# Three-block transformer in one Trainium2 kernel: the second half of the compressed keys and values computed inside the attention's first steps

## The chip, the cores and the metric

The kernel runs on one core of a Trainium2 chip. The metric is the device time of one execution in microseconds. The kernel before was timed three times: 2164.24, 2169.11 and 2172.72 us, median 2169.11 us. TensorE (PE) multiplies, VectorE (DVE) and ScalarE (ACT) work element by element, GpSimd (POOL) and SyncE (SP) mostly issue transfers here. Each engine runs its own program in order, and the programs meet at semaphores.

## The reference, cut to what matters

The input is 512 tokens of 1024 features. Three blocks follow one another: a mixed recurrent and linear-attention block, a retention block, and a block with native sparse attention (NSA); each ends with a feed-forward layer. Everything is float32. The change is in the shared keys and values of the third block and in the start of its attention:

```
kv = rms_norm_2(h, kv_norm) @ kv_w
k_c, v_c, k_s, v_s, k_w, v_w = [t.reshape(B, S, G, d) for t in jnp.split(kv, 6, axis=-1)]

def compress(t, pe, w1, w2):              # t: 512 tokens, 4 groups, 64 features
    blocks = t[:, blk_idx] + pe[:, None, :]           # 31 overlapping windows of 32 tokens, step 16
    blocks = blocks.transpose(0, 1, 3, 2, 4).reshape(B, n_cmp, G, CMP_LEN * d)
    return jax.nn.silu(blocks @ w1) @ w2              # 2048 -> 256 -> 64

kc = compress(k_c, cmp_pe_k, cmp_w1_k, cmp_w2_k)
vc = compress(v_c, cmp_pe_v, cmp_w1_v, cmp_w2_v)
```

The attention then has three branches per head: over the 31 compressed keys (kc, vc), over selected blocks, and over a window; each is a masked softmax with a relative bias, and sigmoid gates weigh their sum. With 512 tokens the selected blocks and the window cover all keys before the query, so both are dense causal attentions. Heads: 16 in 4 groups of 64 features.

## The kernel before, in words

Features lie on partitions, so activations are tiles of 128 features by 512 tokens. Every matrix product is made in three passes of float32r: each operand is split into a high part and a low rest (AH and AL of the input, WH and WL of the weights), and a "part" is the three matmuls AH·WH, AL·WH and AH·WL of one 128x128 weight block (L413 for feature tiles, L462 for token tiles). A tile has 8 parts, 24 matmuls.

Weights come in units of 512 KB. SP loads a unit into RAW (three slots), ACT copies it to WH (L883), DVE subtracts and writes WL (L1319). `ahead(u)` makes these copies up to unit u; `before(name, m)` is `ahead` of that tile's unit plus LOOK = 2. ACT may write WH of unit v only when PE has finished unit v-3.

The plan gives each tile one of PSUM banks 0 to 3 in turn. Its order here is: `kv_t` 0 to 7 (features of k_c, v_c, and of k_s and k_w), `kv_v` (tokens: v_s and v_w; four banks at once), `nsa_t` 8 (gates), `nsa_t` 0 to 7 (queries, two heads to a tile; 1 to 7 in bank 7). A tile enters its bank only when the former tenant was read out (L394).

- The evacuation of `kv_t` 0 to 3 (L1376) writes CK. `kv_t` 4 to 7 go to T[n % 4], ACT and DVE spread each over KHH and KLL (L1205 to L1206, L1799 to L1800).
- DVE sets KCH, KCL and VC to zero ahead of CK (L1782 and L1783).
- `windows(i)` (L1803) builds X2, the blocks of half i: eight copies of 64x496 (L1812) and then one addition of the position embedding to all of X2 (L1816). Half 0 is made between `kv_tile(5)` and `kv_tile(6)` in DVE's program, half 1 after `kv_v`. 
- `hidden(i)` (L734) is blocks @ w1: 32 float32 matmuls of 124 columns, each of which leaves two records. `hidden_act(i)` (L1227) is the SiLU on ACT, `compressed(i)` (L749, L751) the product with w2. Half 0 stands between `kv_v` and `nsa_t` 8, half 1 between `nsa_t` 8 and `nsa_t` 0. POOL loads the second w1 into the same W1 when hidden(0) is done (L379).
- DVE copies the compressed values into VC (L1839).

The attention is a loop of steps written out by hand, the same step number s on PE, ACT and DVE (L845, L1252, L1952). Step s is one head, one block of 128 queries (order 0, 3, 1, 2) and one branch: steps 0 to 3 have 128 keys, 4 to 7 512, 8 to 11 256, 12 to 15 384. In step s PE transposes the weights of step s-9 (`turn`, L821, banks 2, 3 and 6 in rotation), computes the scores of s (L806 and L807, banks 0 and 1 in rotation), and every fourth step from 14 on the values (L839). DVE adds the bias and takes the maximum (L1927) into the ring SS, ACT takes the exponential (L1267), DVE weighs (L1950) the step s-6, ACT copies turned weights (L1259). The compressed branch has its own small scores (L791 and L792, 16 pairs), first in step 2. Parts of the next query tile are spread over steps: parts 4 to 7 of `nsa_t` 1 in steps 0 to 3, `nsa_t` 2 in steps 6 to 13. `query(n)` on DVE (L1845, L1852) and `query_high(n)` on ACT (L1203) turn a query tile into QHL: n = 1 stands in step 4, n = 2 in step 15. Ahead of the loop DVE also makes the gates (L1857, L1860) and a memset of CS8 (L1863).

Of the kernel before, what the change touches and what calls it, by code (L numbers as in the profile page):

```python
# [14 lines left out]
S = 512  # L15
# [7 lines left out]
LOOK = 2  # L23
# [6 lines left out]
    ("gla_norm", 1), ("pe_k", 16), ("pe_v", 16),  # L30
# [46 lines left out]
def plan():  # L77
    p = Plan()
    for m in OPEN_IN + (11, 8, 9, 2, 3):
        p.tile("w_in_t", m)  # L80
    p.tokens("w_in_v", 0)
    for m in (12, 13, 14, 15, 4, 5, 6, 7):
        p.tile("w_in_t", m)
    for m in range(8):
        p.tile("w_out", m)

    def ffn(n):
        for m in range(44):
            p.tile(f"ffn{n}_in", m)
        for m in range(8):  # L90
            p.tile(f"ffn{n}_out", m)

    ffn(1)
    for h in range(4):
        for m in range(4):
            p.tile("ret_t", 8 * h + m)
        p.tokens("ret_v", h)
        for j in range(4):
            p.bank["scores", h, j] = p.turn()
        for m in range(4, 8):  # L100
            p.tile("ret_t", 8 * h + m)
    for m in range(8):
        p.tile("ret_out", m)
    ffn(2)
    for m in range(8):
        p.tile("kv_t", m)
    p.tokens("kv_v", 0)
    for m in (8, 0):
        p.tile("nsa_t", m)
    for m in range(1, 8):  # L110
        p.tile("nsa_t", m, bank=7)
    for m in range(8):
# [33 lines left out]
def build(nc, D, out):  # L146
    p = plan()
    n_units = len(p.units)
    with ExitStack() as ctx:
# [24 lines left out]
        sb("origin", [128, 96])  # L174
# [41 lines left out]
        with ExitStack() as ar:  # L216
            TT = [sb(f"TT{i}", [128, 4, S], stack=ar) for i in range(2)]
            KHH = sb("KHH", [128, 8, S], F32R, ar)
            KLL = sb("KLL", [128, 8, S], F32R, ar)
            VS = sb("VS", [128, 4, 512], stack=ar)  # L220
            GT = sb("GT", [128, 4, 48], stack=ar)
            KCH = sb("KCH", [128, 4, 32], F32R, ar)
            KCL = sb("KCL", [128, 4, 32], F32R, ar)
            VC = sb("VC", [128, 4, 4, 64], stack=ar)
            with ExitStack() as ac:
                CK = sb("CK", [128, 4, S], stack=ac)
                X2 = sb("X2", [128, 16, 124], stack=ac)
                W1 = sb("W1", [128, 16, 256], stack=ac)
                HC = sb("HC", [128, 2, 124], stack=ac)
                W2 = sb("W2", [128, 2, 2, 128], stack=ac)  # L230
            QHL = [sb(f"QHL{i}", [128, 4, S], F32R, ar) for i in range(2)]
            SS = [sb(f"SS{i}", [128, S], stack=ar) for i in range(8)] + SQ
            PT = [sb(f"PT{i}", [128, S], stack=ar) for i in range(5)] + [ACC]
            NM = sb("NM", [128, 8], stack=ar)
            SM = sb("SM", [128, 4, 4], stack=ar)
            CF = sb("CF", [128, 4, 4], stack=ar)
            CM = sb("CM", [128, 3, 8], stack=ar)
# [73 lines left out]
        def query_after(s):  # L311

            return {4: 1, 15: 2}.get(s, s // PAIR + 1 if 2 * PAIR <= s <= 6 * PAIR and s % PAIR == 0 else None)

        def queries_before(s):

            return {4: 2}.get(s, s // PAIR + 2 if PAIR <= s < 6 * PAIR and s % PAIR == 0 else None)

        def queries_in(s):

            if s < 4:
                return 1, s + 4
# [28 lines left out]
        def pool_program(e):  # L351
# [36 lines left out]
        def tensor_program(e):  # L388
# [338 lines left out]
            def hidden(i):  # L727
                for ht in range(2):
                    enter(4 + ht, ("hidden", i, ht))
                    if ht == 0:  # L730
                        e.wait_ge(s_w1, 16 * (i + 1))
                        e.wait_ge(*kv_v.at(("x2", i)))
                    for lp in range(16):
                        t = e.matmul(BANK[4 + ht][:, 0:124], W1[:, lp, ht * 128:ht * 128 + 128], X2[:, lp, :],  # L734
                                     start=lp == 0, stop=lp == 15)
                    t.then_inc(matmul.did(("hidden", i, ht)))

            def compressed(i):
                b = 6 + i
# [26 lines left out]
            for kk in range(4):  # L766
                part("nsa_t", 1, kk, A)
# [77 lines left out]
            for s in range(LAST):  # L845
                if TURN <= s < N + TURN:
                    turn(s - TURN)
                if s < N:
                    scores(s)
                for f in range(8):  # L850
                    if s == small_at(f):
                        small_scores(f)
                    if s == small_at(f) + 7:
                        small_turn(f)
                if s >= VALUES and (s - VALUES) % 4 == 0:
                    values((s - VALUES) // 4)
                if queries_in(s):
                    part("nsa_t", *queries_in(s), A)
# [12 lines left out]
        def scalar_program(e):  # L871
# [360 lines left out]
            e.wait_ge(*set_v.at("kc"))  # L1232
# [5 lines left out]
            hidden_act(1)  # L1238

            def query_high(n):  # L1240
                g = n // 2
                e.wait_ge(*free_v.at(("nsa_t", n)))
                if g > 1:
                    e.wait_ge(*matmul.at(("att", GROUP * (g - 1) - 1)))
# [4 lines left out]
            e.wait_ge(*matmul.at(("cmp", 1)))  # L1249
            query_high(0)  # L1250
            before("nsa_t", 1)
            for s in range(LAST + 3):  # L1252
# [8 lines left out]
                if s < N:  # L1261
# [47 lines left out]
        def vector_program(e):  # L1309
# [471 lines left out]
            for k in (KCH, KCL):  # L1781
                e.memset(k[:, :, :].bitcast(F32), 0.0).then_inc(set_v.did("kc"))  # L1782
            e.memset(VC[:, :, :, :], 0.0).then_inc(set_v.did("vc"))  # L1783

# [18 lines left out]
            def windows(i):  # L1803

                for g in range(4):
                    e.wait_ge(*free_v.at(("kv_t", 2 * i + g // 2)))
                    for par in range(2):
                        src = CK[64 * (g % 2):64 * (g % 2) + 64, 2 * i + g // 2, :]
                        win = bass.AP(src.tensor, src.offset + par, [src.ap[0], [2, 16], [16, 31]])
                        if i == 1 and g == 0 and par == 0:  # L1810
                            e.wait_ge(*matmul.at(("hidden", 0, 1)))
                        e.tensor_copy(X2[64 * par:64 * par + 64, :, 31 * g:31 * g + 31], win).then_inc(  # L1812
                            kv_v.did(("pairs", i)))
                pe = V("pe_k" if i == 0 else "pe_v", 0, 16).rearrange("p (l o) -> p l o", o=1)
                e.wait_ge(*kv_v.at(("pairs", i)))
                e.tensor_tensor(X2[:, :, :], X2[:, :, :], pe.broadcast_to([128, 16, 124]), ALU.add).then_inc(  # L1816
                    kv_v.did(("x2", i)))

            for n in range(6):
                kv_tile(n)  # L1820
            windows(0)
            kv_tile(6)
            kv_tile(7)
            before_tokens("kv_v", 0)
            for f in range(8):
                low("q", f, "mix_pre1")
            windows(1)
# [8 lines left out]
            e.wait_ge(*matmul.at(("cmp", 1)))  # L1836
            e.wait_ge(*set_v.at("vc"))
            for i in range(4):
                e.tensor_copy(VC[32 * i:32 * i + 31, i, :, :],  # L1839
                              BANK[7][0:31, 0:256].rearrange("p (g d) -> p g d", g=4)).then_inc(free_v.did(("cmp", 1)))  # L1840

            def query(n):
# [13 lines left out]
            e.wait_ge(*matmul.at("gates"))  # L1856
            e.tensor_copy(GT[:, :, :], BANK[6][:, 0:192].rearrange("p (a b) -> p a b", a=4)).then_inc(  # L1857
                free_v.did("gates"))
            e.wait_ge(*free_v.at("gates"))
            e.reciprocal(GT[:, :, :], GT[:, :, :]).then_inc(set_v.did("gates"))  # L1860
            before("nsa_t", 1)
            e.wait_ge(*kv_v.at(("k", 3)))
            e.memset(CS8, NEG).then_inc(set_v.did("small"))  # L1863
# [15 lines left out]
            def small_scores(f):  # L1879
# [4 lines left out]
                e.wait_ge(*set_v.at("small"))  # L1884
# [176 lines left out]
def laid_out(inp):  # L2061
# [13 lines left out]
        "pe_k": a["cmp_pe_k_2"].reshape(16, 128).T, "pe_v": a["cmp_pe_v_2"].reshape(16, 128).T,  # L2075
    }
# [56 lines left out]
```

## Time and profile before

| what | value |
|---|---|
| median of three runs | 2169.11 us (2164.24 to 2172.72) |
| profiled execution | 2173.35 us, its span 2171.5 us |
| PE busy | 2088.9 us (96%) |
| DVE busy | 1033.1 us (48%) |
| ACT busy | 820.2 us (38%) |
| POOL busy | 12.7 us (1%) |
| mean granted TensorE clock | 0.978 |
| chain that ended last | PE 88%, DVE 6%, ACT 4%, issue 1% |

The span is the time from the first to the last instruction; the execution takes 1.85 us more than that. Times in the rows are microseconds from the span's start. `[1.74 <-DVE CK L1376]` behind a row says that the engine stood idle for 1.74 us before it, and that a write of CK by DVE at line 1376 released it. Ends of matmuls are modelled: a matmul of 512 columns is shown as 0.39 us, while the next starts 0.227 us after it. The granted clock has two levels, 1.00 (2.4 GHz) and 0.50 (1.2 GHz).

### The profile page before, as it was taken

Reading aid. Unit: us, or ns where it says so; the run is one execution under the profiler, and the core shown is the slowest. Engines: PE = TensorE matmul, PEld = TensorE weight load, DVE = VectorE, ACT = ScalarE, POOL = GpSimd, SP = SyncE. Lnnn points to the kernel's source line nnn. Section 1 sums busy time; section 2 is a strip of 40 time slices with the busy share of each in tenths; the row PEclk is TensorE's granted clock in tenths of the full one; section 3 lists DMA queues with packets and bytes.
Section 4 is the critical chain, followed back from the end, with each engine's and each line's share of the span. In section 5 each row is a group of like instructions: output and inputs, shape, how many; then the busy total and the mean of one; then the engine's idle time right before and its main releaser. Section 6 shows DMA issues by size and latency. Waiting matters only on the chain.

```text
span 2171.5 us, 25460 instructions
## 1 busy us (share of the span) xinstructions
PE 2088.9 (96%) x10172; PEld 1711.2 (79%) x10172; DVE 1033.1 (48%) x1705; ACT 820.2 (38%) x1290; POOL 12.7 (1%) x24
## 2 busy tenths in 40 slices
PE   7799999999999999999999999999899999999997
PEld 6578788888887787788788888777788778888886
DVE  4645444443344353342644442275677635444323
ACT  4563333333323233233433322234577634333221
POOL 0000000000000000000000000000000000000000
PEclk9999999999999999999999999999899999999998
DMA  4212233333331221223232333433111022332331
GB/s 134 68 59 78 85 100 97 97 92 100 100 104 45 92 97 54 87 88 97 68 97 97 97 92 97 131 102 107 40 40 40 3 86 78 97 97 97 90 97 66
DMA packets 51812, 184.38 MB, mean 85 GB/s; under 512 B 5818, under 2 KB 6090, under 8 KB 51440
## 3 DMA queue, kind: packets, MB, share of 16 engines
q1 hardware_dynamic: 49248, 171.99, 25.4%
q0 software_dynamic: 2160, 10.63, 1.5%
q8 instruction: 81, 1.33, 0.2%
q14 instruction: 35, 0.29, 0.0%
q10 hardware_dynamic: 288, 0.15, 0.0%
HBM read 180.61 MB, written 2.14 MB: 84 GB/s over the span
## 4 chain that ended last, share of the span: by engine, by line
PE 88%; DVE 6%; ACT 4%; issue 1%; DMA 0%; SPq 0%; DVEq 0%; ACTq 0%
PE bank L413 71%; PE bank L462 6%; PE bank L839 2%; PE bank L700 1%; DVE WL L1319 1%; PE bank L821 1%; PE bank L806 1%; PE bank L690 1%; PE bank L807 1%; PE bank L513 1%; ACT WH L883 1%; PE bank L479 1%; PE bank L596 0%; DVE MF L1650 0%; DMA RAW<-in_w_in_t 0%
## 5 line engine op out<-in xcount | busy, mean ns | idle before, releaser
L1319 DVE TENSOR_TENSOR WL<-RAW,WH 128x1024 fp32r<-128x1024 f32 (+1 forms) x326 | 391.5, 1205 | 579.8 <-ACT WH L883 579.0
L413 PE MATMUL bank<-AH,WH 128*128 128x512 f32 x1584 | 628.4, 400 | 25.7 <-ACT AH L893 15.5
L413 PE MATMUL bank<-AL,WH 128*128 128x512 f32 x1584 | 622.5, 396 | 3.5 <-DVE AL L1337 3.5
L413 PE MATMUL bank<-AH,WL 128*128 128x512 f32 x1584 | 618.9, 394 | 1.9 <-DVE WL L1319 1.9
L883 ACT ACTIVATE WH<-RAW 128x1024 fp32r<-128x1024 f32 (+1 forms) x326 | 338.1, 1041 | 583.6 <-PE bank L413 503.7
L413 PEld LDWEIGHTS bank<-AH,WH 128*128 128x128 f32 x1584 | 302.2, 191 | 94.1 <-issue 20.4
L413 PEld LDWEIGHTS bank<-AL,WH 128*128 128x128 f32 x1584 | 301.8, 191 | 69.6 <-DVE AL L1337 9.6
L413 PEld LDWEIGHTS bank<-AH,WL 128*128 128x128 f32 x1584 | 302.3, 191 | 66.7 <-DVE WL L1319 2.8
L413 PE MATMUL bank<-HH,WL 128*128 128x512 f32 x528 | 205.4, 389 | 0.0
L413 PE MATMUL bank<-HH,WH 128*128 128x512 f32 x528 | 205.4, 389 | 0.0
L413 PE MATMUL bank<-HLO,WH 128*128 128x512 f32 x528 | 205.4, 389 | 0.0
L1376 DVE TENSOR_TENSOR T<-bank,RS 128x512 f32<-128x512 f32 x156 | 106.6, 686 | 162.0 <-PE bank L413 162.0
L413 PEld LDWEIGHTS bank<-HH,WH 128*128 128x128 f32 x528 | 99.1, 188 | 20.7
L413 PEld LDWEIGHTS bank<-HH,WL 128*128 128x128 f32 x528 | 99.1, 188 | 20.6
L413 PEld LDWEIGHTS bank<-HLO,WH 128*128 128x128 f32 x528 | 99.1, 188 | 20.5
L1096 ACT ACTIVATE T<-T 128x512 f32<-128x512 f32 x66 | 41.7, 632 | 127.2 <-DVE T L1376 127.2
L1101 ACT ACTIVATE HH<-T 128x512 fp32r<-128x512 f32 x66 | 41.7, 632 | 125.8 <-DVE T L1622 125.8
L462 PE MATMUL bank<-WH,AH 128*128 128x512 f32 x192 | 76.2, 397 | 6.6 <-DVE XP L1376 4.4
L462 PE MATMUL bank<-WL,AH 128*128 128x512 f32 x192 | 75.8, 395 | 1.6 <-DVE WL L1319 1.6
L462 PE MATMUL bank<-WH,AL 128*128 128x512 f32 x192 | 75.7, 394 | 0.0
L1267 ACT ACTIVATE SS<-SS,NM 128x128 f32<-128x128 f32 (+3 forms) x104 | 58.1, 559 | 28.9 <-DVE NM L1927 28.4
L1624 DVE TENSOR_TENSOR HLO<-T,HH 128x512 fp32r<-128x512 f32 x66 | 45.7, 693 | 46.1 <-ACT HH L1101 46.1
(300 smaller groups left out, 2249.1 us busy)
## 6 DMA issues: line engine op xcount, KB each, us to landing
RAW<-in_ffn_in SPq DMA_DIRECT2D x132, 512.0 KB, 3.5
RAW<-in_ffn_out SPq DMA_DIRECT2D x48, 512.0 KB, 3.5
RAW<-in_ret_t SPq DMA_DIRECT2D x32, 512.0 KB, 3.6
RAW<-in_ffn_out SPq DMA_DIRECT2D x24, 384.0 KB, 3.1
RAW<-in_w_in_t SPq DMA_DIRECT2D x17, 512.0 KB, 3.6
RAW<-in_ret_v SPq DMA_DIRECT2D x16, 512.0 KB, 3.6
RAW<-in_ret_out SPq DMA_DIRECT2D x16, 512.0 KB, 3.6
RAW<-in_nsa_t SPq DMA_DIRECT2D x9, 512.0 KB, 3.5
```

The costliest lines, as they stand in the source:

```text
L413: t = e.matmul(BANK[b][:, :], wt[:, sl], xx[:, slot(kk) if name == "nsa_out" else kk, :], start=kk == 0 and n == 0, stop=kk == kt - 1 and ...
L462: t = e.matmul(BANK[b][:, :], xx[:, kk, tt * 128:(tt + 1) * 128], wt[:, sl], start=kk == 0 and n == 0, stop=kk == 7 and n == 2)
L479: t = e.matmul(BANK[4][:, 4 * tt + q:4 * tt + q + 1], SQ[1][:, ROWS[tt]], ones[:, :], start=True, stop=True)
L513: t = e.matmul(BANK[5][:, ROWS[tt]], src[:, at + tt:at + tt + 1].broadcast_to([128, 128]), ident[:, :], start=True, stop=True)
L839: e.matmul(out[hh], VS[:, j, c:c + 64], PT[(4 * u + 2 * br + hh) % NPT][:, ROWS[j]], start=br == 0 and j == 0, stop=False)
L883: e.activation(WH[v % W_SLOTS][:, 0:n], RAW[v % RAW_SLOTS][:, 0:n], ACT.Copy).then_inc(w_high.did(v))
L1096: e.activation(a[:, :], a[:, :], ACT.Silu).then_inc(gate_a.did((n, j)))
L1101: e.activation(HH[n][:, j, :], T[2 * (j % 2)][:, :], ACT.Copy).then_inc(hid_a.did((n, j)))
L1267: e.activation(scores, scores, ACT.Exp, bias=NM[:, s % 8:s % 8 + 1], scale=-1.0, accum_out=SM[:, u % 4, 2 * hh + br:2 * hh + br + 1]).then ...
L1319: e.tensor_tensor(WL[w][:, 0:n], RAW[r][:, 0:n], WH[w][:, 0:n], ALU.subtract).then_inc(w_low.did(v))
L1376: e.tensor_tensor(dst, BANK[p.bank[name, m]][:, :], RS[:, :], ALU.mult).then_inc(free_v.did((name, m)))
L1624: e.tensor_tensor(HLO[n][:, j, :], a[:, :], HH[n][:, j, :], ALU.subtract).then_inc(hid_v.did((n, j)))
```

## The change

1. `kv_t` 4 and 5 go to banks 6 and 7. So the turn of banks 0 to 3 moves by two for everything behind them: `kv_t` 6 and 7 get banks 1 and 2, `kv_v` 3, 0, 1, 2, `nsa_t` 8 and 0 banks 3 and 0, `nsa_out` and the last feed-forward layer are moved by two as well.
2. The zeroes of KCH, KCL, VC and the memset of CS8 go from DVE to POOL.
3. The blocks of half 0 are built after `kv_tile(7)`, one group at a time between the weight units of `kv_v`. Copy and addition become one instruction: eight additions of 64x496 per half. For it the vector table has two more entries of 16 columns, the embeddings with their halves swapped.
4. hidden(1) is issued in steps 0 to 5 of the attention, six matmuls in each (two in step 5); compressed(1) in step 9, into bank 5; ACT's hidden_act(1) in step 7; DVE's copies to VC in step 11. compressed(0) stays where it was. 
5. `nsa_t` 1 is computed whole ahead of the loop. `query(1)` moves from step 4 to 3, `query(2)` from 15 to 14; `before("nsa_t", 1)` to step 1, `before("nsa_t", 2)` from step 4 to 7. The gates are made in step 2 on DVE.
6. HC and W2 no longer share room with the later buffers; the ring SS has 9 buffers, not 10.

```
-            p.tile("kv_t", m)
+            p.tile("kv_t", m, bank={4: 6, 5: 7}.get(m))
...
-                HC = sb("HC", [128, 2, 124], stack=ac)
-                W2 = sb("W2", [128, 2, 2, 128], stack=ac)
...
-            SS = [sb(f"SS{i}", [128, S], stack=ar) for i in range(8)] + SQ
+            SS = [sb(f"SS{i}", [128, S], stack=ar) for i in range(6, 9)]
+            SS = [sb(f"SS{i}", [128, S], stack=ar) for i in range(4)] + SQ + SS
+            HC = sb("HC", [128, 2, 124], stack=ar)
+            W2 = sb("W2", [128, 2, 2, 128], stack=ar)
...
         def query_after(s):
...
-            return {4: 1, 15: 2}.get(s, s // PAIR + 1 if 2 * PAIR <= s <= 6 * PAIR and s % PAIR == 0 else None)
+            return {3: 1, 14: 2}.get(s, s // PAIR + 1 if 2 * PAIR <= s <= 6 * PAIR and s % PAIR == 0 else None)
...
         def queries_before(s):
...
-            return {4: 2}.get(s, s // PAIR + 2 if PAIR <= s < 6 * PAIR and s % PAIR == 0 else None)
+            return {1: 1, 7: 2}.get(s, s // PAIR + 2 if PAIR <= s < 6 * PAIR and s % PAIR == 0 else None)
...
         def queries_in(s):
...
-            if s < 4:
-                return 1, s + 4
...
             e.dma_start(W2[:, :, :, :], D["cmp_w2"]).then_inc(s_w2, 16)
+            for k in (KCH, KCL):
+                e.memset(k[:, :, :].bitcast(F32), 0.0).then_inc(zeroed.did("kc"))
+            e.memset(VC[:, :, :, :], 0.0).then_inc(zeroed.did("vc"))
...
+            e.wait_ge(*kv_v.at(("k", 3)))
+            e.memset(CS8, NEG).then_inc(zeroed.did("small"))
             e.wait_ge(*matmul.at(("hidden", 0, 1)))
...
-            hidden(0)
+            for ht in range(2):
+                hidden(0, ht, range(16))
             compressed(0)
-            q_split = split_of("q")
-            tile("nsa_t", 8, A, q_split)
-            hidden(1)
-            compressed(1)
+            tile("nsa_t", 8, A, split_of("q"))
             tile("nsa_t", 0, A)
...
-            for kk in range(4):
-                part("nsa_t", 1, kk, A)
+            tile("nsa_t", 1, A)
...
+                if s < 6:      
+                    for lp in range(6 * s, min(6 * s + 6, 32)):
+                        hidden(1, lp // 16, (lp % 16,))
+                if s == 9:
+                    compressed(1)
...
-            hidden_act(1)
...
                 e.wait_ge(*free_v.at(("nsa_t", n)))
+                if n == 0:
+                    e.wait_ge(*kv_v.at(("x2", 1)))
...
+                if s == 7:
+                    hidden_act(1)
...
-                        e.tensor_copy(X2[64 * par:64 * par + 64, :, 31 * g:31 * g + 31], win).then_inc(
-                            kv_v.did(("pairs", i)))
-                e.tensor_tensor(X2[:, :, :], X2[:, :, :], pe.broadcast_to([128, 16, 124]), ALU.add).then_inc(
-                    kv_v.did(("x2", i)))
+                        e.tensor_tensor(X2[64 * par:64 * par + 64, :, 31 * g:31 * g + 31], win,
+                                        pe.rearrange("p (l o) -> p l o", o=1).broadcast_to([64, 16, 31]),
+                                        ALU.add).then_inc(kv_v.did(("x2", i)))
-            for n in range(6):
+            for n in range(8):
                 kv_tile(n)
-            windows(0)
-            kv_tile(6)
-            kv_tile(7)
-            before_tokens("kv_v", 0)
+            for g in range(4):
+                ahead(p.first["kv_v", 0] + g + LOOK)
+                windows(0, (g,))
...
+                if s == 2:
+                    gates()
+                if s == 11:
+                    compressed_values()
```

## Rows read from the trace of the kernel before

**Rows 1.** The page, part 4: the chain that ended last, by engine.
```profile
PE 88%; DVE 6%; ACT 4%; issue 1%; DMA 0%; SPq 0%; DVEq 0%; ACTq 0%
```

**Rows 2.** Timeline of PE, kv_t and kv_v: start, length, instruction, count [idle before <-releaser].
```profile
1440.26 1.98 PE L413 MATMUL bank<-AH,WL 128*128 128x512 f32 x8
1443.98 0.50 PE L413 MATMUL bank<-AH,WH 128*128 128x512 f32 x1 [1.74 <-DVE CK L1376]
...
1468.12 0.50 PE L462 MATMUL bank<-WL,AH 128*128 128x512 f32 x1 [1.63 <-DVE WL L1319]
...
1474.30 0.50 PE L462 MATMUL bank<-WH,AH 128*128 128x512 f32 x1 [2.23 <-DVE T L1376]
```

**Rows 3.** Timeline of DVE in the same stretch.
```profile
1442.47 0.91 DVE L1783 MEMSET VC<- 128x1024 f32 x1 [0.16 <-issue]
...
1459.56 5.12 DVE L1812 COPY X<-CK 64x496 f32<-64x496 f32 x8
1464.71 2.23 DVE L1816 TENSOR_TENSOR X<-X,vec 128x1984 f32<-128x1984 f32 x1
...
1473.56 0.68 DVE L1376 TENSOR_TENSOR T<-bank,RS 128x512 f32<-128x512 f32 x1
```

**Rows 4.** Timeline of PE from hidden(0) to step 11.
```profile
1492.12 7.30 PE L734 MATMUL bank<-X,W 128*128 128x124 f32 x64
...
1507.58 7.38 PE L734 MATMUL bank<-X,W 128*128 128x124 f32 x64 [0.20 <-issue]
1515.42 1.05 PE L751 MATMUL bank<-W,HC 128*31 128x64 f32 x16 [0.46 <-ACT HC L1227]
...
1525.32 0.22 PE L806 MATMUL bank<-KHH,QHL 128*128 128x128 f32 x1
...
1528.24 0.33 PE L806 MATMUL bank<-KHH,QHL 128*128 128x128 f32 x1 [0.94 <-DVE NM L1927]
...
1530.27 0.48 PE L413 MATMUL bank<-AH,WH 128*128 128x512 f32 x1
...
1539.18 0.79 PE L806 MATMUL bank<-KHH,QHL 128*128 128x512 f32 x1 [3.22 <-DVE NM L1927]
...
1548.20 0.27 PE L821 MATMUL bank<-ident,SS 128*128 128x128 f32 x1
```

**Rows 5.** Timeline of DVE, VC to step 5.
```profile
1516.51 1.75 DVE L1839 COPY VC<-bank 31x256 f32<-31x256 f32 x4 [7.72 <-PE bank L751]
...
1525.33 1.35 DVE L1860 RECIPROCAL GT<-GT 128x192 f32<-128x192 f32 x1
...
1534.08 0.69 DVE L1845 SCALAR_TENSOR_TENSOR T<-bank,RS 128x512 f32<-128x512 f32 x1
1535.56 1.41 DVE L1852 TENSOR_TENSOR QHL<-T,QHL 64x512 fp32r<-64x512 f32 x2 [0.80 <-ACT QHL L1203]
1537.30 1.23 DVE L1319 TENSOR_TENSOR WL<-RAW,WH 128x1024 fp32r<-128x1024 f32 x1 [0.33 <-ACT WH L883]
```

**Rows 6.** Timeline of ACT: table load, SiLU, weight copy, exponential.
```profile
1509.48 1.28 ACT L1227 ACT_TABLE_LOAD   x1
1511.43 0.27 ACT L1227 ACTIVATE HC<-bank 128x124 f32<-128x124 f32 x1 [0.67 <-PE bank L734]
...
1536.21 1.06 ACT L883 ACTIVATE WH<-RAW 128x1024 fp32r<-128x1024 f32 x1
...
1539.88 0.71 ACT L1267 ACTIVATE SS<-SS,NM 128x512 f32<-128x512 f32 x1
```

**Rows 7.** Stretches: us, busy PE, PEld, DVE, ACT, POOL (count), granted clock, DMA share, GB/s.
```profile
1534.00:1540.00 6.00, 2.78 (x8) 1.85 (x8) 4.81 (x12) 4.16 (x9) 0.00 (x0) 0.78 0.09 10
1540.00:1550.00 10.00, 10.00 (x50) 8.54 (x50) 6.75 (x30) 5.18 (x17) 0.00 (x0) 0.74 0.13 48
...
1600.00:1620.00 20.00, 19.39 (x167) 15.94 (x161) 16.13 (x55) 15.78 (x44) 0.00 (x0) 1.00 0.09 27
```

**Rows 8.** Timeline of POOL, the memset at the start.
```profile
0.74 0.95 POOL L352 MEMSET bd<- 128x1024 f32 x1 [0.29 <-POOLq L2125]
```

More of the change, by code:

```diff
@@ L29 @@
     ("conv_w", 16), ("conv_b", 4), ("lru_ba", 4), ("lru_bi", 4), ("lru_lambda", 4), ("b_alpha", 2),
-    ("gla_norm", 1), ("pe_k", 16), ("pe_v", 16),
+    ("gla_norm", 1), ("pe_k", 16), ("pe_v", 16), ("pe_k_swapped", 16), ("pe_v_swapped", 16),
 ]
@@ L173, in build @@
         sums = sb("sums", [128, 4])
-        sb("origin", [128, 96])
+        sb("origin", [128, 64])
         BANK = [ctx.enter_context(nc.psum_tensor(f"bank{i}", [128, 512], F32)) for i in range(8)]
@@ L725, in tensor_program, with hidden @@
             tokens("kv_v", 0, A)
[L727 to L736, printed above, removed]
+            def hidden(i, ht, lps):
+                b = 4 + ht
+                for lp in lps:
+                    if lp == 0:
+                        enter(b, ("hidden", i, ht))
+                        if ht == 0:
+                            e.wait_ge(s_w1, 16 * (i + 1))
+                            e.wait_ge(*kv_v.at(("x2", i)))
+                    t = e.matmul(BANK[b][:, 0:124], W1[:, lp, ht * 128:ht * 128 + 128], X2[:, lp, :], start=lp == 0,
+                                 stop=lp == 15)
+                    if lp == 15:
+                        t.then_inc(matmul.did(("hidden", i, ht)))
             def compressed(i):
-                b = 6 + i
+                b = 6 - i
                 enter(b, ("cmp", i))
@@ L1231, in scalar_program @@
             e.wait_ge(*matmul.at(("cmp", 0)))
-            e.wait_ge(*set_v.at("kc"))
+            e.wait_ge(*zeroed.at("kc"))
             e.activation(KCH[:, :, 0:31], BANK[6][:, 0:128].rearrange("p (g n) -> p g n", g=4)[:, :, 0:31],
@@ L1248, in scalar_program @@
             before("nsa_t", 0)
-            e.wait_ge(*matmul.at(("cmp", 1)))
             query_high(0)
-            before("nsa_t", 1)
             for s in range(LAST + 3):
@@ L1778, in vector_program @@
             fourth("kv_t", 3, "kv", False)
-            for k in (KCH, KCL):
-                e.memset(k[:, :, :].bitcast(F32), 0.0).then_inc(set_v.did("kc"))
-            e.memset(VC[:, :, :, :], 0.0).then_inc(set_v.did("vc"))
             def kv_tile(n):
@@ L1801, in kv_tile, with windows @@
                         kv_v.did(("k", k)))
-            def windows(i):
-                for g in range(4):
+            def windows(i, gs):
+                for g in gs:
                     e.wait_ge(*free_v.at(("kv_t", 2 * i + g // 2)))
+                    own = slice(64 * (g % 2), 64 * (g % 2) + 64)
                     for par in range(2):
-                        src = CK[64 * (g % 2):64 * (g % 2) + 64, 2 * i + g // 2, :]
+                        src = CK[own, 2 * i + g // 2, :]
                         win = bass.AP(src.tensor, src.offset + par, [src.ap[0], [2, 16], [16, 31]])
+                        pe = V(("pe_k", "pe_v")[i] + ("" if g % 2 == par else "_swapped"), 0, 16)[own]
                         if i == 1 and g == 0 and par == 0:
                             e.wait_ge(*matmul.at(("hidden", 0, 1)))
-                        e.tensor_copy(X2[64 * par:64 * par + 64, :, 31 * g:31 * g + 31], win).then_inc(
-                            kv_v.did(("pairs", i)))
-                pe = V("pe_k" if i == 0 else "pe_v", 0, 16).rearrange("p (l o) -> p l o", o=1)
-                e.wait_ge(*kv_v.at(("pairs", i)))
-                e.tensor_tensor(X2[:, :, :], X2[:, :, :], pe.broadcast_to([128, 16, 124]), ALU.add).then_inc(
-                    kv_v.did(("x2", i)))
-            for n in range(6):
+                        e.tensor_tensor(X2[64 * par:64 * par + 64, :, 31 * g:31 * g + 31], win,
+                                        pe.rearrange("p (l o) -> p l o", o=1).broadcast_to([64, 16, 31]),
+                                        ALU.add).then_inc(kv_v.did(("x2", i)))
+            for n in range(8):
                 kv_tile(n)
-            windows(0)
-            kv_tile(6)
-            kv_tile(7)
-            before_tokens("kv_v", 0)
+            for g in range(4):
+                ahead(p.first["kv_v", 0] + g + LOOK)
+                windows(0, (g,))
             for f in range(8):
                 low("q", f, "mix_pre1")
-            windows(1)
+            windows(1, range(4))
             e.wait_ge(*kv_a.at("kc"))
@@ L1835, in vector_program, with compressed_values @@
                 free_v.did(("nsa_t", 8)))
[L1836 to L1840, printed above, removed]
+            def compressed_values():
+                e.wait_ge(*matmul.at(("cmp", 1)))
+                e.wait_ge(*zeroed.at("vc"))
+                for i in range(4):
+                    e.tensor_copy(VC[32 * i:32 * i + 31, i, :, :],
+                                  BANK[5][0:31, 0:256].rearrange("p (g d) -> p g d", g=4)).then_inc(free_v.did(("cmp", 1)))
             def query(n):
@@ L1855, in vector_program, with gates @@
             query(0)
[L1856 to L1863, printed above, removed]
+            def gates():
+                e.wait_ge(*matmul.at("gates"))
+                e.tensor_copy(GT[:, :, :], BANK[6][:, 0:192].rearrange("p (a b) -> p a b", a=4)).then_inc(
+                    free_v.did("gates"))
+                e.wait_ge(*free_v.at("gates"))
+                e.reciprocal(GT[:, :, :], GT[:, :, :]).then_inc(set_v.did("gates"))
             def by_head(t):
@@ L1883, in small_scores @@
                 e.wait_ge(*matmul.at(("small", f)))
-                e.wait_ge(*set_v.at("small"))
+                e.wait_ge(*zeroed.at("small"))
                 if f > 0:
@@ L2075, in laid_out @@
         "pe_k": a["cmp_pe_k_2"].reshape(16, 128).T, "pe_v": a["cmp_pe_v_2"].reshape(16, 128).T,
+        "pe_k_swapped": a["cmp_pe_k_2"].reshape(16, 2, 64)[:, ::-1].reshape(16, 128).T,
+        "pe_v_swapped": a["cmp_pe_v_2"].reshape(16, 2, 64)[:, ::-1].reshape(16, 128).T,
     }
```

## The prediction

> **What bounds the kernel now.** Read the chain of the page first: PE holds 88% of what ended last, DVE 6% [rows 1]. Shortening DVE or ACT work is worth only what it takes from PE's waits, so the next view is PE's timeline around the edits, with the idle time in brackets. Between the last matmul of `kv_t` 3 and hidden(0) PE waits three times: 1.74 us for the evacuation of bank 1 (CK), 1.63 us for WL, 2.23 us for the evacuation of `kv_t` 7's bank [rows 2]. In the attention's first steps it waits 0.94 and 3.22 us for DVE's maximum [rows 4]. The stretches then show what a timeline hides: from 1534 to 1540 PE is busy 2.78 of 6 us, and its granted clock is 0.78 there and 0.74 in the next 10 us, against 1.00 in the running attention [rows 7]. Everything behind step 11 I expect to shift as a block.
>
> **kv_t and kv_v (edits 1 to 3).** PE issues 96 matmuls of `kv_t` 4 to 7 and 96 of `kv_v` between 1442.24 (1440.26 + 1.98) and 1492.12: 49.9 us [rows 2, 4]. The last 78 of them run without a wait from 1474.30 to 1492.12, 17.82 us, with 0.11 us for the restart: 0.227 us each [rows 2, 4]. 192 x 0.227 = 43.6 us. So 6.3 us can go. Does it?
> - `kv_t` 4 enters bank 6, which no one has read from lately, and its weight rests are written ahead: no wait, so DVE's memsets (0.91 us for VC, two more of some 0.17) and the CK evacuations no longer stand in the way [rows 3]. On POOL the same size took 0.95 us [rows 8]; there it runs behind the load of w1, while PE is at the sums after the feed-forward, some 35 us ahead of the first use. The bounds are 0 and, if POOL disturbed DVE for all three, 1.3 us; I take 0.
> - The windows no longer precede the weight rest of `kv_v` 0: DVE goes from `kv_tile(5)` straight to it and writes it near 1459, PE needs it at 1442.1 + 96 x 0.227 = 1463.9. Before, 5.12 + 2.23 us stood ahead of it [rows 3].
> - `kv_v`'s first two bank groups use banks 3 and 0, long read out; the third and fourth use those of `kv_t` 6 and 7 and begin 2.7 and 4.1 us after 1463.9, and DVE reads `kv_t` 7 out by about 1465.5. No wait.
> - What is late next: X2. One addition of 64x496 I take at 0.67 us, just under the 0.68 us of 512 columns [rows 3]; no row shows it with this stepped source and broadcast vector; the ends are 0.64 (5.12 / 8, the copy of that shape) and 1.31 (copy and addition one behind the other). ACT can write the weight unit of `nsa_t` 0 only when PE has done the third unit of `kv_v`, 1463.9 + 16.3 = 1480.2; 1.06 us for it, 1.23 for DVE's rest [rows 5, 6], two additions: 1483.9. PE needs X2 at 1485.7. Even at 1.31 us each it is 1485.1. Covered, by 1.8 us.
> So hidden(0) starts near 1485.7 in place of 1492.1: **-6.3 us**. hidden(0), compressed(0) and `nsa_t` 8 follow as before (ACT's high parts and its table load end before hidden(0) does).
>
> **From nsa_t 8 to step 11 (edits 4 and 5).** Before, `nsa_t` 8 ends at about 1507.4 and the turn of step 11 begins at 1548.20: 40.8 us [rows 4]. I place the new order in time, with `nsa_t` 8 ending at 1501.0. X2 of half 1 starts when hidden(0) is read, 1493, and takes 5.4 us in place of 7.3, so it is ready 14 us before its use; w1's second load likewise.
> - `nsa_t` 0, the gate transposes, all of `nsa_t` 1: 5.45 + 0.4 + 5.45 us. att 0 at 1512.3 (before: 1525.32 with only four parts of `nsa_t` 1 done). DVE's query(0), 2.9 us, is hidden by the 5.45.
> - PE, steps 0 to 5: hidden(1) is 7.3 us of unchanged matmuls [rows 4], 1.37 us a step; scores 0.25 us at 128 keys and 0.46 at 512; small scores 1.8 (the part behind them begins at 1530.27, the scores ahead at 1528.24) [rows 4]. PE is through step 5 at 1523.2.
> - DVE, steps 0 to 3: step 1 gains a weight rest behind ACT's copy (to 1517.3), step 2 the gates, 0.34 + 1.35 us [rows 5], and small scores (to 1520.4), step 3 maximum, shift and query(1), 0.69 + 0.75 waiting + 1.41 [rows 5] (to 1523.9). Maximum 4 ends at 1524.5. att 6 needs its bank: **PE waits 1.4 us** at step 6, in place of 0.94 + 3.22.
> - Steps 6 to 8 on PE, 3 x 0.69 of parts and the scores, to 1528.0; step 9's turn and scores follow, small turn to 1529.0.
> - Step 9's compressed(1) needs ACT: exp 7 ends at 1529.0, then a table load 1.28, two SiLUs 0.54 [rows 6]: 1530.8. **PE waits 1.85 us**, then 1.05 us of work [rows 4].
> - Behind the SiLUs ACT makes the weight copy of step 7 (1.06), until 1531.9, and DVE waits for it from 1528.6, then needs 1.23: maximum 8 ends at 1533.5. **PE waits 0.8 us** for att 10, and 0.25 for the small scores' bank.
> - Step 10 ends and step 11's turn begins at 1536.7.
>
> 1548.2 - 1536.7 = 11.5 us in all, 5.2 of them here. The exponential's table is loaded again (1.28 us), ACT catches up: exp 8 to PT 0 by 1534.4, and the bank of turn 0 is wanted at 1536.7. VC's four copies, 1.75 us [rows 5], come in step 11 on DVE. Their cover is the two score banks: PE issues att s two steps ahead of need, DVE idles about 0.5 us a step there. The lag reaches att 14 just as it is due: 0, at most 1.75; I take 0.1. Moving query(2) by a step, 0, from -1 to +1.
>
> Here a rule of the Trainium skill speaks against the change. The row: the SiLU's load took 1.28 us, ended at 1510.76, and the next activation began at 1511.43 after 0.67 us in which it waited for PE [rows 6], so nothing longer than 0.67 us hid behind it. "ScalarE: Activation LUTs", section "What ACT_TABLE_LOAD costs", puts a switch at about 2.66 us, with a drain of 1.38 us beside the load. By it the two switches in steps 7 and 8 would cost PE 1.4 us more at step 9, and the sum would be 1.4 us smaller. By the row it isn't; the trace disagrees.
>
> **The clock.** My times above are at 1.00. In the profile the granted clock from 1534 to 1550 is short of full by 0.22 x 6 and 0.26 x 10 us: 7.8 us at its lower level, 0.50 [rows 7], around and behind PE's idle 3.22 us. They are inside the 40.8. The new stretch is fuller up to step 5 (hidden(1) is dense) but has 1.4, 1.85 and 1.05 us of waiting and small matmuls from step 6 to 10. Bounds: no slow spell (0), or as much as before (7.8 us, half of it lost where PE is busy: 4). I take one spell and a bit, **+2 us**, nearest to the before.
>
> **Sum.** -6.3 - 5.2 + 0.1 + 2 = -9.4 us. The profiled execution, 2173.35 us (span 2171.5 and 1.85 around it), becomes 2163.9; the median of the runs is 4.2 us below the profiled one, 2169.11 - 9.4 = 2159.7. The larger vector table (128 x 128 bytes more at the start) and the 9-buffer ring cost nothing in the sum.
>
> **Rivals.**
> - *A, the clock stays full or DVE's waits come out shorter*: -11.5 and a little of DVE's slack, -13: 2156. For it: hidden(1) fills the steps where the clock fell. Against: three waits remain between steps 6 and 10.
> - *B, the start of the attention only trades its waits*: ACT's two table loads and the weight copy behind them stall DVE and PE longer than I placed, slow spells as before: -5.2 becomes -1; -6.3 - 1 + 2 = -5.3, 2163.8, the case reaching from -4 to -7.5. For it: three engines hand over to each other in steps 7 to 10. Against: before, PE waits 4.2 us there as well.
> - *C, slower*: the ring of 9. DVE's maximum s now waits for turn s-9, not s-10; if that bound each of the remaining 119 steps by 0.2 us it cost 24 us, 2184. It turns the sum at 9.4 / 119 = 0.08 us a step. Against: in PE's order turn s-9 stands right before att s, for which DVE waits anyway.
> - *D, the change does not remove kv's waits* (ACT's weight copies, which wait for PE's units, are the next bound there): -3, 2166. Against: the margins above, 1.8 us and more.
>
> **How the numbers follow.** Forecast, -7.5 to -12: 0.55. A: 0.20. B: 0.13. D: 0.06. C: 0.06. What this measurement can tell from no change is 0.5%, 10.8 us: 2158.3. A lies beyond it, and of the forecast case the fourth or third between -10.8 and -12 (0.18): faster 0.38. Slower by over 0.5% is C, less its lower half where it only eats the gain, and an unlucky median: 0.05. The rest, 0.57, is within. The range: up to B and most of D, 2167; down to A's far side with the 4 us by which runs differ, 2152.
>
> **What would show it.** kv stretch: PE from 1442.2 to hidden(0) without a wait, 43.6 us. att 0 near 1512.3. Waits at steps 6, 9 and 10 of 1.4, 1.85 and 0.8 us, the second released by ACT's HC. DVE's long wait in step 7, for WH. The turn of step 11 near 1537 to 1539. From there to the end the same length as before. I am wrong if PE waits for X2 or WL before 1486, if the waits of steps 6 to 10 exceed 6 us together, or if the steady steps grow.

## The result and the profile after

The changed kernel took 2155.69 us in the median of 16 runs (2153.99 to 2165.82), the kernel before 2169.72 us in 16 runs (2164.02 to 2173.55). The ratio is 0.9949, 95% interval [0.9936, 0.9963]: 11.1 us faster, from 8.0 to 13.9. The medians stand 14 us apart because the times of the changed kernel lie in heaps, eight of the 16 at 2154.0 to 2154.7 and three at 2165.3 to 2165.8; the ratio weighs all of them. The forecast was 9.4 us less, 2159.7 us, within 2152 to 2167. The profiled execution took 2161.55 us, its span 2159.7 against 2171.5.

The page, part 4, of the changed kernel answers to [rows 1]: a little more of the end is PE's.

```profile
PE 89%; DVE 5%; ACT 4%; issue 1%; DMA 0%; SPq 0%; DVEq 0%; ACTq 0%
```

PE's timeline of `kv_t` 4 to hidden(0) answers to [rows 2] and the first of [rows 4]. The stretch has no bracket at all: `kv_t` 4 starts 0.23 us behind the last matmul of `kv_t` 3, and hidden(0) comes 43.5 us later.

```profile
1440.50 1.98 PE L418 MATMUL bank<-AH,WL 128*128 128x512 f32 x8
1442.32 0.39 PE L418 MATMUL bank<-AH,WH 128*128 128x512 f32 x1
...
1485.84 7.30 PE L740 MATMUL bank<-X,W 128*128 128x124 f32 x64
```

POOL's and DVE's timelines there answer to [rows 8] and [rows 3]. The zeroes are done at 1405.74, 36 us before DVE begins to write CK (1442.18). The additions, two per group, took 1.03 us each and not 0.67; the last ends at 1485.06, 0.8 us before PE reads X2.

```profile
1404.48 0.22 POOL L375 MEMSET KCH<- 128x128 f32 x1
...
1404.77 0.97 POOL L376 MEMSET VC<- 128x1024 f32 x1
```

```profile
1470.26 2.06 DVE L1821 TENSOR_TENSOR X<-CK,vec 64x496 f32<-64x496 f32 x2
...
1483.00 2.06 DVE L1821 TENSOR_TENSOR X<-CK,vec 64x496 f32<-64x496 f32 x2
```

PE in the attention's first steps, the answer to [rows 4]: att 0, then the waits of steps 6, 9 and 10, the turn of step 11, att 16, and att 17 with a wait that the forecast did not have.

```profile
1512.44 0.22 PE L810 MATMUL bank<-KHH,QHL 128*128 128x128 f32 x1
...
1524.20 0.50 PE L810 MATMUL bank<-KHH,QHL 128*128 128x512 f32 x1 [0.84 <-DVE NM L1932]
...
1530.36 1.05 PE L758 MATMUL bank<-W,HC 128*31 128x64 f32 x16 [1.66 <-ACT HC L1236]
...
1532.81 0.39 PE L810 MATMUL bank<-KHH,QHL 128*128 128x256 f32 x1 [0.40 <-DVE NM L1932]
...
1535.94 0.27 PE L825 MATMUL bank<-ident,SS 128*128 128x128 f32 x1
...
1542.53 0.30 PE L810 MATMUL bank<-KHH,QHL 128*128 128x128 f32 x1
...
1546.42 0.33 PE L810 MATMUL bank<-KHH,QHL 128*128 128x128 f32 x1 [3.23 <-DVE NM L1932]
```

ACT in steps 7 and 8 (answer to [rows 6]): load, two SiLUs, weight copy, load. The load starts 0.01 us behind the end of the accumulator read that closes the exponential, and the first SiLU 0.02 us behind the load.

```profile
1528.28 0.19 ACT L1275 ACTIVATION_READ_ACCUMULATOR SS<-SS,NM 128x1 f32 x1
1528.48 1.28 ACT L1236 ACT_TABLE_LOAD   x1
1529.78 0.44 ACT L1236 ACTIVATE HC<-bank 128x124 f32<-128x124 f32 x2
1530.10 1.06 ACT L892 ACTIVATE WH<-RAW 128x1024 fp32r<-128x1024 f32 x1
1531.18 1.28 ACT L1275 ACT_TABLE_LOAD   x1
```

DVE behind it (answer to [rows 5]): its wait for WH in step 7, VC's copies in step 11, the maximum of step 14, query(2), and only then the maximum of step 15, on which att 17 waits. From VC's copies (1536.84) to the start of query(2) (1543.03) the timeline shows no idle time of DVE.

```profile
1531.19 1.23 DVE L1329 TENSOR_TENSOR WL<-RAW,WH 128x1024 fp32r<-128x1024 f32 x1 [3.04 <-ACT WH L892]
...
1536.84 1.75 DVE L1845 COPY VC<-bank 31x256 f32<-31x256 f32 x4
...
1541.11 0.55 DVE L1932 CUSTOM_DVE_ANT_0 SQ<-bank,TT 128x384 f32<-128x384 f32 x1
...
1543.03 0.64 DVE L1851 SCALAR_TENSOR_TENSOR T<-bank,RS 128x512 f32<-128x512 f32 x1
1544.37 1.41 DVE L1858 TENSOR_TENSOR QHL<-T,QHL 64x512 fp32r<-64x512 f32 x2 [0.69 <-ACT QHL L1212]
1545.80 0.56 DVE L1932 CUSTOM_DVE_ANT_0 SS<-bank,TT 128x384 f32<-128x384 f32 x1
```

The stretches answer to [rows 7]. The granted clock is full until the wait of step 17 and falls behind it.

```profile
1534.00:1540.00 6.00, 6.00 (x41) 5.28 (x40) 5.01 (x18) 2.06 (x10) 0.00 (x0) 1.00 0.16 63
1540.00:1550.00 10.00, 6.52 (x46) 5.19 (x45) 7.59 (x23) 7.76 (x19) 0.00 (x0) 0.86 0.01 2
```

Since single executions differ by several us where the kernels are the same, the experiments are read by stretches of one profile each, from the start of one matmul to the start of another. The number in brackets says for how many of these us the granted clock was at its lower level. "both halves" is the changed kernel run again (e4_same).

| from ... to, us | before | after | e1, kv alone | e2, attention alone | both halves |
|---|---|---|---|---|---|
| kv_t 0 to hidden(0) | 80.2 (3.6) | 74.4 (6.0) | 73.7 (3.9) | 80.3 (4.1) | 73.7 (4.2) |
| hidden(0) to att 0 | 33.2 (0) | 26.6 (0) | 33.5 (0) | 26.6 (0) | 26.6 (0) |
| att 0 to turn of step 11 | 22.9 (10.2) | 23.5 (0) | 22.9 (10.2) | 23.5 (0) | 23.6 (0.3) |
| ... to att 16 | 6.6 (0) | 6.6 (0) | 6.6 (0) | 8.1 (3.4) | 8.0 (3.1) |
| att 16 to att 20 | 9.6 (3.4) | 11.0 (3.4) | 9.5 (3.4) | 9.0 (0) | 10.6 (3.4) |
| att 20 to att 96 | 116.3 (0) | 116.3 (0) | 116.3 (0) | 116.3 (0) | 116.4 (0) |
| att 96 to nsa_out | 51.9 (6.8) | 50.7 (3.4) | 52.0 (6.8) | 50.7 (3.4) | 49.1 (0) |
| kv_t 0 to nsa_out | 320.7 | 309.1 | 314.5 | 314.6 | 308.1 |

### The profile page after: what moved, and what is told of

Its sections match the earlier page's. It is cut to its first block, busy times and chain, and to the rows that moved or that the text cites. A ratio compares the mean times of both kernels' runs of the same rounds, so it can differ in the third digit from the quotient of the medians.

```text
span 2159.7 us, 25460 instructions
## 1 busy us (share of the span) xinstructions
PE 2084.8 (97%) x10172; PEld 1709.4 (79%) x10172; DVE 1033.3 (48%) x1699; ACT 820.3 (38%) x1291; POOL 14.3 (1%) x28
## 4 chain that ended last, share of the span: by engine, by line
PE 89%; DVE 5%; ACT 4%; issue 1%; DMA 0%; SPq 0%; DVEq 0%; ACTq 0%
PE bank L418 72%; PE bank L467 6%; PE bank L843 2%; PE bank L705 1%; PE bank L825 1%; DVE WL L1329 1%; PE bank L695 1%; PE bank L518 1%; PE bank L810 1%; PE bank L811 1%; PE bank L484 1%; ACT WH L892 1%; DMA RAW<-in_w_in_t 0%; PE bank L601 0%; DVE SS L1932 0%
```

## The experiments

The theory: two separate gains, 6 us in `kv_t` and `kv_v` and 4 to 5 us at the start of the attention, where some 3 us are given back at step 17. The rivals: the gains need each other, or the clock makes them.

**e1_kv and e2_attention: the change in two halves.** e1 is the kernel before with edits 1 to 3, e2 the kernel before with edits 4 to 6; the memset of CS8, which is in edit 2, went with e2.

> Edits 1 to 3 alone in the kernel before: kv_t 4 and 5 in banks 6 and 7, zeroes of KCH, KCL and VC on POOL, blocks built by eight additions between the weight units of kv_v. The start of the attention is as before. My theory: no wait between kv_t 3 and hidden(0), that stretch 43.6 us in place of 49.9, and 6 us less in the whole (2163.5). The rival, that the two halves of the change only work together or that the clock decides: less than 3 us, because the granted clock falls elsewhere.

> Edits 4 to 6 alone (hidden(1) in steps 0 to 5, compressed(1) in step 9, nsa_t 1 whole ahead of the loop, gates and VC in the loop, ring of 9, CS8 on POOL); kv_t's banks, the zeroes and the blocks as before. My theory: the three waits of kv_t and kv_v stay (1.7, 1.6 and 2.2 us), the turn of step 11 comes 5 to 6 us earlier than before, about 3 us of it is given back at step 17, and the whole is 4 to 5 us faster (2165). The rival, that the attention's gain is all given back at step 17 and that the rest of the 11 us measured is kv and clock: within 1.5 us of the kernel before.

e1: ratio 0.9968 [0.9952, 0.9984], 6.9 us; from `kv_t` 0 to hidden(0) 6.5 us less at nearly the same clock. Behind it one thing is new: PE waits 0.52 us for X2 ahead of hidden(1), because eight additions of half 1 take longer (8.3 us in the changed kernel) than copies and addition did (7.35), and hidden(0) to att 0 is 0.3 us longer than before. The theory holds. e2: its three kv waits stay at 1.74, 1.64 and 2.23 us, and the waits of steps 6, 9 and 10 are those of the changed kernel (0.84, 1.66, 0.40). By its trace it is 6.1 us shorter from `kv_t` 0 to `nsa_out`, of which 1.2 lie behind att 96, where only the ring is shorter and the clock was low for 3.4 us less. By its runs it is 0.9992 [0.9978, 1.0005], 1.7 us: the upper end, 4.8 us, just takes in the theory; alone the timing does not show this half. The two differences, 6.2 and 6.1, add up to 12.3, against 11.5 and 12.6 in the two profiles of both together, and the timed 6.9 and 1.7 to 8.6, against 8.7 in e4. So neither half needs the other, but for the 0.3 us that the additions cost in e1 and that edit 4 hides.

How much of the attention half reaches the whole time is open: the trace says 6.1 us, the runs at most 4.8. In this stretch e2's profile has 13 us less at the lower clock than the profile before; over whole runs the mean granted clock is 0.9806 (twelve runs) against 0.9799 (25 runs of the kernel before), only about 3 us less. So the lower clock seems to come back in other places of the kernel, at a cost that the stretches do not see; that this is the whole gap is not shown.

**e4_same: the changed kernel again.**

> The changed kernel itself, as the measure for the others of this chip. Expected 11 us (0.5%) below the kernel before, PE's waits at steps 6, 9, 10 and 17 as in the first profile within 0.2 us, the granted clock's lower spells in other places.

Ratio 0.9960 [0.9946, 0.9974]: 8.7 us, where 11 were expected. The waits are 0.83, 1.65 and 0.40 us; that of step 17 is 2.76 and not 3.23, as the clock was low before it (3.1 us between the turn of step 11 and att 16, which made 8.0 us of 6.6) and DVE had caught up meanwhile. So the spells of lower clock do move from run to run, and the wait at step 17 with them.

**e5_banks and e6_windows_late: which edit removes which kv wait.**

```
-        p.tile("kv_t", m)
+        p.tile("kv_t", m, bank={4: 6, 5: 7}.get(m))
```

```
-            for n in range(6):
+            for n in range(8):
                 kv_tile(n)
             windows(0)
-            kv_tile(6)
-            kv_tile(7)
```

> The kernel before with kv_t 4 and 5 in banks 6 and 7 and nothing else. My theory: of PE's three waits the first (1.74 us, for CK) and the third (2.23, for the evacuation of kv_t 7) go, because both are bank waits; the second (1.63, for WL behind the windows) stays: the way from kv_t 4 to hidden(0) 45.5 us or so, against 43.5 with all edits. The rival, that the third wait is really ACT's and DVE's queue and only takes another name: it stays near 2 us, now for WL.

> The kernel before with windows(0) behind kv_tile(7), in its old form of eight copies and one addition, and nothing else. My theory: the WL wait and the wait for kv_t 7's bank go (the second was the windows' delay passed on) down to 0.3 us or so, the wait for CK stays: 45.5 us to hidden(0). The rival, that kv_t 7's bank is late in any case, as its evacuation follows the whole tile: the third wait stays near 1 to 2 us.

PE's waits in the timeline of e5, and below in that of e6:

```profile
1461.44 0.50 PE L462 MATMUL bank<-WL,AH 128*128 128x512 f32 x1 [1.64 <-DVE WL L1319]
1467.61 0.50 PE L462 MATMUL bank<-WH,AH 128*128 128x512 f32 x1 [2.21 <-DVE T L1376]
```

```profile
1439.30 0.50 PE L413 MATMUL bank<-AH,WH 128*128 128x512 f32 x1 [1.74 <-DVE CK L1376]
1474.61 0.50 PE L462 MATMUL bank<-WL,AH 128*128 128x512 f32 x1 [1.92 <-DVE WL L1319]
```

e5: my expectation failed for the third wait. The banks remove only the wait for CK; the wait for `kv_t` 7's bank stays at 2.21 us, because that tile is read out late, behind the windows, whatever its bank. e6 removes both later waits where they were, and gets a new one of 1.92 us further on: the 7.35 us of copies and addition in one piece now stand before the weight rest of `kv_v` 2. From the last matmul of `kv_t` 3 to hidden(0) it is 48.0 us in e5 and 47.7 in e6, where 45.5 were expected of each, against 49.9 before and 43.5 with all edits. So each edit takes what it can (1.9 and 2.2 us), and by difference the last 2.3 us need the windows cut up between the weight units; no run has that edit alone.

**e3_query_15 and e9_values_10: the wait of step 17.**

```
-            return {3: 1, 14: 2}.get(s, s // PAIR + 1 if 2 * PAIR <= s <= 6 * PAIR and s % PAIR == 0 else None)
+            return {3: 1, 15: 2}.get(s, s // PAIR + 1 if 2 * PAIR <= s <= 6 * PAIR and s % PAIR == 0 else None)
```

```
-                if s == 11:
+                if s == 10:
                     compressed_values()
```

> The changed kernel with query(2) back in step 15 (it stands in 14). In the changed kernel PE waits 3.23 us in step 17 for the maximum of step 15, which stands behind VC's copies of step 11 and query(2) of step 14 on DVE. My theory: with one step more between them the wait in step 17 falls to 1.5 us or less and the later wait grows by no more than 1: 1 to 2 us faster than the changed kernel. The rival, that query(2)'s 2.7 us on DVE cost PE the same wherever they stand: the wait moves to step 18, same time within 0.5 us.

> The changed kernel with DVE's copies to VC in step 10, ahead of the small scores for which DVE waits 0.76 us, and not in step 11. My theory: the 3.23 us at step 17 come from VC's 1.75 us and query(2) together; 0.76 us of the copies are hidden, so the wait at step 17 falls by 0.3 to 0.8. The rival, that query(2) alone makes that wait (moved to step 15 it fell to 0.96): it stays at 3.2 within 0.1.

PE's waits behind step 11 in e3, and below in e9:

```profile
1540.55 0.41 PE L818 MATMUL bank<-ident,T 128*128 128x128 f32 x2 [0.25 <-DVE T L1920]
1542.99 0.44 PE L825 MATMUL bank<-ident,SS 128*128 128x128 f32 x2 [0.96 <-ACT PT L1267]
```

```profile
1542.69 0.33 PE L810 MATMUL bank<-KHH,QHL 128*128 128x128 f32 x1 [2.76 <-DVE NM L1932]
1543.38 0.41 PE L818 MATMUL bank<-ident,T 128*128 128x128 f32 x2 [0.25 <-DVE T L1920]
```

With query(2) in step 15 the wait for the maximum is gone, and the kernel before's own 0.96 us for PT comes back. From att 16 to att 20 e3 took 8.4 us (0), e2 with query(2) in step 14 9.0 (0): 0.6 us at full clock. In e2 the clock had been low just ahead, as in e4, and the wait was 2.76 us. With full clock ahead and a spell of 3.4 us inside, the changed kernel took 11.0 us where before took 9.6. With VC's copies a step earlier the wait falls by 0.47 us, at the same full clock up to att 16. Both belong to it. Timed, e3 is 0.9955 [0.9938, 0.9972], which cannot be told from the changed kernel; the 1 to 2 us expected are not shown.

**e7_weights_first and e8_no_silu: what the SiLU in the loop costs.** In e7 ACT has `if s == 6: before("nsa_t", 2)` in its loop; that is the weight unit of `nsa_t` 4.

```
-                    e.activation(HC[:, ht, :], BANK[4 + ht][:, 0:124], ACT.Silu).then_inc(
+                    e.activation(HC[:, ht, :], BANK[4 + ht][:, 0:124], ACT.Silu if i == 0 else ACT.Copy).then_inc(
```

> The changed kernel with ACT's weight copy of step 7 (for nsa_t 3's successor) moved to step 6, ahead of the two SiLUs; DVE's rest stays in step 7. My theory: DVE's wait of 3.04 us for WH in step 7 goes, PE's wait of 0.4 us at step 10 goes, the 1.66 us for HC at step 9 stay: 0.5 to 0.8 us faster by the turn of step 11. The rival, that this copy delays the exponential and so the SiLUs: the wait at step 9 grows by up to 1 us and nothing is won.

> The changed kernel with a plain copy in place of the SiLU of the second half, so that no activation table is changed in steps 7 and 8 (it leaves the SiLU of the compressed values out). My theory: PE's wait at step 9 (1.66 us) falls by 1.28 to 0.4, DVE's wait for WH by the same, both loads together are worth 1.3 to 1.7 us at the turn of step 11. The rival by a drain beside each load: 2.7 us.

PE at step 9 of e7, and below at steps 9 and 10 of e8:

```profile
1523.59 1.05 PE L758 MATMUL bank<-W,HC 128*31 128x64 f32 x16 [1.65 <-ACT HC L1236]
```

```profile
1526.05 1.05 PE L758 MATMUL bank<-W,HC 128*31 128x64 f32 x16 [0.23 <-ACT HC L1236]
1528.50 0.38 PE L810 MATMUL bank<-KHH,QHL 128*128 128x256 f32 x1 [0.40 <-DVE NM L1932]
```

e7: the wait for HC stays, those of DVE for WH and of PE at step 10 go; att 0 to the turn of step 11 takes 22.5 us, 1.0 less (0.5 to 0.8 expected). From there to att 20 it keeps all of it (40.0 against 41.1, both with 3.4 us of lower clock). Timed: 0.9937 [0.9917, 0.9958]. e8: the wait falls by 1.43 us, and the stretch to step 11 by 1.4 to 22.1. Here a switch on PE's path costs its 1.28 us and 0.15 us around it. "ScalarE: Activation LUTs" of the Trainium skill, "What ACT_TABLE_LOAD costs", gives about 2.66 us for every switch, with a drain of 1.38; the trace disagrees.

**e11_two and e10_best: shifts put together.** e11 has e7's and e3's. e10 has also compressed(1) in step 10 and VC's copies in step 12.

> The changed kernel with two of the shifts only: ACT's weight copy in step 6 and query(2) in step 15. If the gains of the single runs add up: 1 us at the turn of step 11 and 0.6 to 1.4 at step 17, 2 us shorter than the changed kernel from att 0 to att 20. If DVE's earlier finish only lengthens its later waits: 1 us.

> The changed kernel with four shifts: ACT's weight copy in step 6, compressed(1) on PE in step 10 behind the small scores, VC's copies on DVE in step 12, query(2) in step 15. My theory: no wait for HC is left, the waits at steps 9 and 10 fall from 2.06 to 0.3 us, that of step 17 to 1: 4 us shorter than the changed kernel from att 0 to att 20, about 0.2% faster. The rival, that VC's copies in step 12 come so near to the values of step 14 that PE waits there: 1.5 us of it are lost.

e11: 39.2 us from att 0 to att 20 against 41.1, both with 3.4 us of lower clock: 1.9 less, about the sum of the single gains (1.0 for e7, 0.6 to 1.4 at step 17). Timed it is 0.9953 [0.9933, 0.9974], so the trace's 1.9 us cannot be seen there. In e10 the waits fall as expected:

```profile
1523.36 0.39 PE L810 MATMUL bank<-KHH,QHL 128*128 128x256 f32 x1 [0.18 <-DVE NM L1934]
1536.90 0.33 PE L810 MATMUL bank<-KHH,QHL 128*128 128x128 f32 x1 [0.56 <-DVE NM L1934]
...
1540.04 0.69 PE L825 MATMUL bank<-ident,SS 128*128 128x128 f32 x2 [0.96 <-ACT PT L1267]
```

But the stretch to att 20 takes 40.8 us, only 0.3 less and not the 4 expected. The clock was at its lower level for 10.2 us of it against 3.4; where PE is busy, these 6.8 us cost up to 3.4. In this profile PE's own waits were traded for a slower PE. Timed it is the lowest of all, 2153.57 us (2150.62 to 2155.47), 0.9928 [0.9904, 0.9953]; the intervals of e7 and of the changed kernel overlap it. It is faster than the kernel before; that it beats the changed one is not shown.

**e12_operands: why an addition took 1.03 us.**

```
+                        if g > 1:
+                            win = CK[own, 2 * i + g // 2, 0:496].rearrange("p (l o) -> p l o", o=31)
+                        added_in = pe.rearrange("p (l o) -> p l o", o=1).broadcast_to([64, 16, 31])
+                        if g % 2:
+                            added_in = RS[own, 0:496].rearrange("p (l o) -> p l o", o=31)
```

> The changed kernel with other operands in the additions that build the blocks, so that the four groups show the four cases (it adds other values, the compressed keys and values are not the reference's): group 0 stepped window and broadcast vector as in the change, group 1 stepped window and a dense tile, group 2 contiguous columns and the broadcast vector, group 3 both dense. In the changed kernel one took 1.03 us, 0.67 was forecast. My theory: the step in the source next to a second operand costs it: groups 0 and 1 near 1.03, 2 and 3 near 0.67. The rival, that the broadcast vector costs it: 0 and 2 near 1.03.

DVE's timeline, groups 0 to 3 of the first half, two additions each:

```profile
1465.54 2.04 DVE L1826 TENSOR_TENSOR X<-CK,vec 64x496 f32<-64x496 f32 x2
...
1468.87 2.05 DVE L1826 TENSOR_TENSOR X<-CK,RS 64x496 f32<-64x496 f32 x2
...
1472.73 1.36 DVE L1826 TENSOR_TENSOR X<-CK,vec 64x496 f32<-64x496 f32 x2
...
1478.29 1.38 DVE L1826 TENSOR_TENSOR X<-CK,RS 64x496 f32<-64x496 f32 x2
```

Stepped 1.02 us, contiguous 0.68, whatever the second operand is. The theory holds.

## Why the prediction was right, point by point

1. *kv_t and kv_v, -6.3 us.* Right: 6.5 us in e1, and all three waits are gone. That X2 was covered by 1.8 us was too wide, it was 0.8: the addition was mis-sized (0.67 for 1.03). My upper end, 1.31, had taken it in. For half 1 the same error turned the sign: 5.4 us in place of 7.3 was forecast, it took 8.3. In the changed kernel hidden(1) comes late enough, in e1 it cost 0.3 us.
2. *hidden(1) into the steps.* att 0 was forecast for 1512.3, came at 1512.44; the waits 1.4, 1.85 and 0.8 us were 0.84, 1.66 and 0.40, on the engines named; the turn of step 11 was to start at 1536.7 and started at 1535.94. The mechanism was right; in place of 5.2 us this part gave 6.0 in the first profile.
3. *VC's copies 0.1 us, query(2) a step earlier 0.* This step failed. In DVE's rows after, query(2) begins 4.4 us behind VC's copies, with no idle time between, so the lag of the first is still there when the second begins: PE waits 3.23 us for the maximum of step 15. Before, DVE still idled 0.5 us in each of steps 13 and 14, and PE's stop near there was 0.96 us, for PT:

```profile
1558.55 0.47 PE L821 MATMUL bank<-ident,SQ 128*128 128x128 f32 x2 [0.96 <-ACT PT L1259]
```

   From att 16 to att 20 the change costs 1.4 us with the clock alike in both profiles (11.0 against 9.6), and 0.6 in e2 against e3, where the wait was shorter. I had looked at each alone and let two score banks cover each.
4. *The clock, +2 us.* In this place it was too much: nothing up to att 16 in the first profile, 1.4 us in e4. The 7.8 us at the lower level that I took from the windows behind 1534 were also too few: from att 0 to the turn of step 11 it was 10.2 before. What the clock gives or takes in the rest of the kernel cannot be settled with these runs.
5. *The rest costs nothing.* att 20 to att 96 takes 116.3 us in both, and no longer than before behind att 96, so the ring of 9 (rival C) costs nothing. POOL's zeroes cost nothing seen: e1 has them and all three kv waits are gone.

Sum: the stretch from `kv_t` 0 to `nsa_out` is 11.5 us shorter in the first profile and 12.6 in e4, the timed gain 11.1 and 8.7, the forecast 9.4. That the sum came so near is in part luck. In the first profile its terms are -5.8 (the clock was low 2.4 us longer there), -6.0, +1.4 and 0, and -1.2 behind att 96 that I had not forecast: the 2 us for the clock did not come, and they partly covered the 1.3 us that step 17 took more than I gave it. By the stretches it is rival A that happened (11.5 and 12.6 us less, full or nearly full clock up to step 11, shorter waits), to which I gave 0.20; the median of the first runs, 2155.69 us, is its 2156 too. I gave 0.38 to faster by over 0.5% and 0.57 to within; the measured 0.51%, from 0.37 to 0.64, lies on that line, so this can't be told.

## What to carry to other kernels

List every wait of the bounding engine with its releaser, lay the new order on the same clock with durations from the rows, and name what is late next: this gave the place of three new waits within 0.8 us. Then check deferred work not edit by edit but together: two small pieces moved onto the same engine within its slack spend that slack once. And where a change of 0.3 to 0.5% is at stake, compare one stretch at a time in profiles at equal granted clock; whole times need more runs than there were. Then hold the sum of the stretches against the timed gain: e2's did not agree.

## What the runs showed of the hardware

- An addition of 64x496 float32 whose source steps by 16 elements took 1.02 us, a contiguous one 0.68 (e12). A copy from the same stepped source took 0.61 us in the median, 0.64 each in the row of eight [rows 3]. "Advanced Engine Details and Errata" of the Trainium skill, "SBUF Cachelines", says that accesses which each fall in another 16-byte line run slower. The additions agree. Whether the copy pays it too is not shown: no contiguous copy of this shape was run, and the nearest one-operand instruction, a TENSOR_SCALAR over 512 contiguous columns, took 0.48 us.
- On one core the same work took longer where the granted clock was lower for longer. The stretch from the retention block's first tile to the second feed-forward layer, which no edit touches, took 431.6 us with 9 us at the lower level in e4 and 436.4 with 20.0 in the first profile of the same kernel: 4.8 us, nearly half of what was to be measured.
